# A streaming encoder layer on one core: the new frames' attention in batches of 512 cached keys, the time mixing without a loop

## The reference, cut to what matters

```python
def rwkv_scan(S0, r, w, k, v, kk, a):
    def step(S, inp):
        r_t, w_t, k_t, v_t, kk_t, a_t = inp
        sa = jnp.einsum('bhvk,bhk->bhv', S, -kk_t)
        S = (S * w_t[:, :, None, :] + sa[..., None] * (kk_t * a_t)[:, :, None, :]
             + v_t[..., None] * k_t[:, :, None, :])
        return S, jnp.einsum('bhvk,bhk->bhv', S, r_t)

def fox_sample_attention(q, k, v, logf, k_past, v_past, logf_past):
...
    lp = logf_past.astype(f32)
    tail = jnp.swapaxes(lax.cumsum(lp, axis=1, reverse=True) - lp, 1, 2)
    s_past = (jnp.einsum('bqhd,bkhd->bhqk', q, k_past.astype(q.dtype)).astype(f32) * SCALE
              + c_new[..., :, None] + tail[..., None, :])
    s_new = (jnp.einsum('bqhd,bkhd->bhqk', q, k).astype(f32) * SCALE
             + c_new[..., :, None] - c_new[..., None, :])
    s_new = jnp.where(jnp.tril(jnp.ones((n, n), bool)), s_new, -jnp.inf)
    p = jax.nn.softmax(jnp.concatenate([s_past, s_new], axis=-1), axis=-1).astype(v.dtype)
    return (jnp.einsum('bhqk,bkhd->bqhd', p[..., :P], v_past.astype(v.dtype))
            + jnp.einsum('bhqk,bkhd->bqhd', p[..., P:], v))
```

## Time and profile before

| | us |
|---|---|
| median of three runs | 4143.74 |
| lowest and highest of the three | 4136.17, 4197.59 |
| the profiled execution | 4199.51 |
| its span, first to last instruction | 4197.7 |

### The profile page before, as it was taken

How to read it: one execution, slowest core, us unless ns; L and a number is a source line. 1 busy time by engine, 2 the same in 40 slices (tenths; PEclk the granted TensorE clock), 3 DMA queues, 4 the chain that set the end, 5 groups by cost and what they waited for, 6 DMA issues and landing times. The chain is left out here.

```text
span 4197.7 us, 81747 instructions
## 1 busy us (share of the span) xinstructions
PE 3837.7 (91%) x30701; PEld 2339.2 (56%) x30702; DVE 1621.2 (39%) x3480; ACT 1007.4 (24%) x1829; POOL 232.7 (6%) x348
## 2 busy tenths in 40 slices
PE   8999989989898989869998988994899999999988
PEld 4444448878788878845554764553333333333333
DVE  1222225656556666657775112336011111111117
ACT  2222223323223333225554121110000000000003
POOL 0000010000000000001110000000000000000005
PEclk9999989999999999979999569996899999999999
DMA  5111120000000000021101132220756656754238
GB/s 201 53 53 53 49 56 2 17 10 17 10 10 17 10 17 10 10 97 51 51 11 49 50 105 77 87 84 15 282 216 273 265 208 261 285 225 185 110 116 313
DMA packets 143285, 420.98 MB, mean 100 GB/s; under 512 B 30744, under 2 KB 73888, under 8 KB 130752
## 3 DMA queue, kind: packets, MB, share of 16 engines
q1 hardware_dynamic: 123472, 345.77, 22.4%
q0 software_dynamic: 11616, 42.21, 2.8%
q10 hardware_dynamic: 7952, 29.36, 1.8%
HBM read 750.60 MB, written 69.36 MB: 195 GB/s over the span
## 5 line engine op out<-in xcount | busy, mean ns | idle before, releaser
L2698 PE MATMUL e_H<-e_w,e_xT 128*64 128x512 f32 x1536 | 686.3, 600 | 19.8 <-DMA e_w<-in_moe_w 16.4
L2699 PE MATMUL e_H<-e_w,e_xT 128*64 x1536 | 686.1, 600 | 0.0
L292 PE MATMUL fp<-f_w,f_xT 128*128 128x512 f32 (+1 forms) x1360 | 533.3, 547 | 9.7 <-DMA f_w<-in_w_in 9.3
L716 PE MATMUL rp_pa<-r_xT,w_rwkv 128*128 128x128 f32 x3808 | 484.0, 281 | 0.7 <-ACT r_xT L1020 0.7
L716 PEld LDWEIGHTS rp_pa<-r_xT,w_rwkv 128*128 128x128 f32 x3808 | 449.9, 193 | 35.3 <-issue 23.0
L2698 PEld LDWEIGHTS e_H<-e_w,e_xT 128*64 128x64 f32 x1536 | 208.1, 138 | 436.2 <-issue 409.6
L292 PEld LDWEIGHTS fp<-f_w,f_xT 128*128 128x128 f32 x1360 | 244.2, 199 | 262.6 <-issue 260.9
L2717 PE MATMUL e_Y<-e_w,e_gT 128*64 128x512 f32 x768 | 339.8, 595 | 1.0 <-DMA e_w<-in_moe_w 1.0
L2718 PE MATMUL e_Y<-e_w,e_gT 128*64 x768 | 339.8, 595 | 0.0
L2717 PEld LDWEIGHTS e_Y<-e_w,e_gT 128*64 128x64 f32 x768 | 101.3, 137 | 197.2 <-issue 189.6
L2699 PEld LDWEIGHTS e_H<-e_w,e_xT 128*64 128x64 f32 x1536 | 208.1, 138 | 0.6
(11 more groups left out here) (404 smaller groups left out, 5580.0 us busy)
## 6 DMA issues: line engine op xcount, KB each, us to landing
e_w<-in_moe_w SPq DMA_DIRECT2D x288, 2048.0 KB
scratch_ypad<-e_y ACTq DMA_DIRECT2D x48, 512.0 KB, 2.7
scratch_h<-m_h SPq DMA_DIRECT2D x17, 512.0 KB, 2.6
z_h<-scratch_h SPq DMA_DIRECT2D x17, 512.0 KB, 7.9
f_x<-in_x_prompt SPq DMA_DIRECT2D x16, 512.0 KB, 3.8
r_x<-in_x_prompt SPq DMA_DIRECT2D x16, 512.0 KB, 3.8
c_kc<-in_cache_fox_k SPq DMA_DIRECT2D x32, 256.0 KB, 2.6
c_v<-in_cache_fox_v SPq DMA_DIRECT2D x1, 8192.0 KB, 25.2
```

The lines of the kernel that those rows point to most:

```text
L292: mm = eng.matmul(out, xT[:, slot, k, :], w[:, k, a:a + n], start=(k == 0), stop=(k == KD - 1))
L716: mm = eng.matmul(pre_bank(bank)[:, f * P:(f + 1) * P], w[:, d, (i + f) * P:(i + f + 1) * P], xT[:, d, :], start=(d == 0), stop=(d == KD - 1))
L2698: eng.matmul(out[lower, :], xT[:, s, k, lower], w[:, SECOND, k, :], start=on, stop=off)
L2699: mm = eng.matmul(out[upper, :], xT[:, s, k, upper], w[:, bass.ds(place, 1), k, :], start=on, stop=off)
```

## The change

The sample's attention is written anew. Keys come in 8 batches of 4 tiles. For each batch PE makes 16 transposes into four PSUM banks (one per pair of heads), ACT and DVE copy two banks each, and PE makes the scores in four products of 512 columns and 64 rows, two per group of heads, on alternate halves of the output. The forget sums inside a tile come from products with the gates spread over the 32 queries of each head (ACT spreads them); sums over whole tiles are added by DVE with the reduction that also finds the smallest value. The exponent is taken in pieces of 1024 keys. Weights are turned two tiles at a time, copied by DVE, and multiplied with the values so that each head of a group writes its own strip of 32 rows; the division by the total is done at the end on the result. The small loads and the first half of the keys are issued by SP in the prompt's attention; the keys go into the buffer that held the first half of the prompt's queries, keys and sums, and w_out takes the same place later. Loads of w_out move from ACT's queue to SP's. The old parts stand in the kernel before; the new ones are cut to their core:

```diff
@@ rwkv: run
-            with eng.Fori(0, NT // 2 - 2) as j:
-                for slot in (0, 1):
-                    tile(2 * j + slot + 2, slot, j + 1)
-            tile(NT - 2, 0, NT // 2 - 1)
-            tile(NT - 1, 1, NT // 2 - 1)
+            for t in range(2, NT):
+                tile(t, t % 2, t // 2)
@@ fox_prompt
+        shared = keep["shared"]
+        q = [shared[:, 0:SEQ], sb("a_q", [P, SEQ])[:, :]]
+        k = [shared[:, SEQ:2 * SEQ], sb("a_k", [P, SEQ])[:, :]]
...
+                if j == 1:
...
+                        sp.dma_start(keep["c_lf"][:, :, :], io["cache_fox_logf"][0, 0].rearrange("(n p) h -> p n h", p=P))\
+                          .then_inc(keep["sample_loaded"], 16)
+
+            sp.wait_ge(reduced, last_read[PAIRS - 2, NT - 1][1])
+            for n in range(4):
+                sp.dma_start(shared[:, n * SEQ:(n + 1) * SEQ].rearrange("p (n c) -> p n c", c=DG),
+                             io["cache_fox_k"][0, 0].rearrange("(n p) h d -> p n (h d)", p=P)[:, 4 * n:4 * n + 4, :])\
+                  .then_inc(keep["early_keys_loaded"], 16)
@@ fox_sample, SP
+            keys(EARLY)
+            keys(EARLY + 1)
+            values(0)
+            keys(EARLY + 2)
+            keys(EARLY + 3)
+            values(1)
+            for n in (2, 3):
+
+                sp.wait_ge(scored, BATCHES * (n - 1))
+                values(n)
+            sp.dma_start(keep["w_out"], io["w_out"][0].rearrange("(c p) n -> p c n", p=P)).then_inc(keep["w_out_loaded"], 16)
+            sp.wait_ge(turned_done, PAIRS * (EARLY + 3))
+            sp.dma_start(vnew, io["s_v"]).then_inc(vnew_loaded, 16)
@@ fox_sample, PE
+            def tails(b):
...
+                for g in (0, 1):
+                    for n in range(BT):
+                        eng.matmul(score[b % 2][g][:, n * P:(n + 1) * P], gates[:, b * BT + n, g, :], keep["after"][:, :],
+                                   start=(n == 0), stop=False)
+
+            def scores(b):
...
+                for a in range(PAIRS):
+                    eng.wait_ge(*copied(b, a))
+                    half = slice(a % 2 * DH, (a % 2 + 1) * DH)
+                    mm = eng.matmul(score[b % 2][a // 2][half, :], qbd[:, a, :], kT[:, b % 2, a, :], start=False, stop=True)
...
+            for b in range(BATCHES):
+                if b > 0:
+                    tails(b)
+                scores(b)
+                if b + 1 < BATCHES:
+                    turn(b + 1)
+            new_scores()
...
+            def values(d):
...
+                    for h in range(HEADS):
+                        g, s = divmod(h, HG)
+                        at = i * 256 + g * P + s * NEW
+                        mm = eng.matmul(score[1][g][s * NEW:(s + 1) * NEW, 0:DH], pT[0:w, d % 3, at:at + NEW],
+                                        (v[:, n, :] if n < CT else vnew)[:, h * DH:(h + 1) * DH], start=(n == 0), stop=(n == CT))
...
+            turn_p(0)
+            turn_p(1)
+            for d in range(len(p_copied_all)):
+                if d + 2 < len(p_copied_all):
+                    turn_p(d + 2)
+                values(d)
@@ fox_sample, ACT
+            eng.wait_ge(lowest_made, 1)
+            for c in range(PAST // EXP):
+                m = EXP if (c + 1) * EXP < PAST else EXP + NEW
+                for g in (0, 1):
+                    eng.activation(z[:, g, c * EXP:c * EXP + m], z[:, g, c * EXP:c * EXP + m], ACT.Exp, scale=-1.0,
+                                   bias=lowest[:, g:g + 1], accum_out=total[:, g, c:c + 1]).then_inc(exped, 1)
```

More of the change, by code:

```diff
@@ L1650, in scores @@
                             eng.wait_ge(reduced, unit_free[n - 2][e])
-                        eng.matmul(score[n % 2][e][:, 0:m], q[rows, par, t * P:(t + 1) * P],
-                                   k[rows, par, c * 512:c * 512 + m], start=True, stop=True).then_inc(scored, 1)
+                        eng.matmul(score[n % 2][e][:, 0:m], q[par][rows, t * P:(t + 1) * P],
+                                   k[par][rows, c * 512:c * 512 + m], start=True, stop=True).then_inc(scored, 1)
             def turn(j, b, i):
@@ L1955, in _ @@
-            turn(0, 0, 0)
-            with eng.Fori(0, CT // 2 - 1) as j:
-                for s in (0, 1):
-                    turn(2 * j + s + 1, 1 - s, j + s)
-                    keys(2 * j + s, s)
-            turn(CT - 1, 1, CT // 2 - 1)
-            keys(CT - 2, 0)
-            keys(CT - 1, 1)
-            eng.wait_ge(*kact.after("s", CT - 1))
-            keys(CT, 0, past=False)
-            eng.matmul(bank[5][0:NEW, :], zeros[0:NEW, :], v[0:NEW, CT, :], start=True, stop=False)
-            eng.wait_ge(v_loaded, 16)
@@ new lines, in new_scores @@
+            def new_scores():
+                eng.wait_ge(reduced, 2 * (BATCHES - 1))
+                eng.wait_ge(made, 6)
+                for g in (0, 1):
+                    out = score[BATCHES % 2][g]
+                    eng.matmul(out[:, 0:NEW], pick[:, g, :], negc[:, :], start=True, stop=False)
+                    eng.matmul(out[:, 0:NEW], spread[:, :], keep["causal"][0:NEW, 0:NEW], start=False, stop=False)
+                    for i in (0, 1):
+                        mm = eng.matmul(out[i * DH:(i + 1) * DH, 0:NEW], qbd[:, 2 * g + i, :], knew[:, 2 * g + i, :],
+                                        start=False, stop=True)
+                    mm.then_inc(scored, 1)
@@ new lines, in _ @@
+            eng.wait_ge(keep["sample_loaded"], 64)
+            for h in range(HEADS):
+                mm = eng.matmul(score[1][0][0:CT, h:h + 1], lf[:, :, h], keep["ones"][:, 0:1], start=True, stop=True)
+            mm.then_inc(totalled, 1)
+            turn(0)
+            tails(0)
+            eng.wait_ge(tot_copied, 1)
+            for g in (0, 1):
+                mm = eng.matmul(score[1][1][:, g * CT:(g + 1) * CT],
+                                tot[:, g, :], keep["after"][0:CT, 0:CT], start=True, stop=True)
@@ L2015, in keys @@
-            def keys(n, s):
-                eng.wait_ge(*kpe.after("s", n))
-                eng.copy(logit[:, :, bass.ds(n * P, P)], bank[4][:, 0:2 * P].rearrange("p (g t) -> p g t", g=2))\
-                   .then_inc(*kact.done("s"))
-            turned_keys(0, 0)
-            with eng.Fori(0, CT // 2 - 1) as j:
-                for s in (0, 1):
-                    turned_keys(2 * j + s + 1, 1 - s)
-                    keys(2 * j + s, s)
-            turned_keys(CT - 1, 1)
-            keys(CT - 2, 0)
@@ new lines, in copies @@
+            def copies(b):
+                for a in range(1, PAIRS, 2):
+                    eng.wait_ge(turned_done, PAIRS * b + a + 1)
+                    if b > 1:
+                        eng.wait_ge(scored, 2 * (b - 1))
+                    eng.tensor_copy(kT[:, b % 2, a, :], turned[a][:, :]).then_inc(dve_copied, 1)
+            copies(0)
+            eng.wait_ge(summed, 1)
+            eng.tensor_copy(cum[:, :, :], score[1][1][:, 0:2 * CT].rearrange("p (g n) -> p g n", g=2)).then_inc(cum_copied, 1)
@@ L2993, in build @@
         keep = constants(nc, ctx)
-        for name in ("w_rwkv", "w_out"):
+        for name in ("w_rwkv", "w_out", "sample", "early_keys"):
             keep[name + "_loaded"] = ctx.enter_context(nc.semaphore(name + "_loaded"))
```

378 lines of the change are left out of this document (187 added, 191 removed).

## The result

The changed kernel takes **3970.6 us** (median of four runs, 3966.2 to 3976.0) against 4148.9 (4136.2 to 4197.6) beside it: ratio **0.951, 95% interval 0.944 to 0.957**. The forecast was 3982. The profiled execution took 3973.5 us, its span is 3971.7.

The account below looks back on a forecast made before the run. TensorE (PE) was taken to bound nearly all of the program, with the sample attention the odd one. From the profiled 4199.5 us, 51.2 (time mixing) and 166.3 (sample attention) were subtracted, giving 3982 us, range 3925 to 4045.

Parts of the forecast that it names:

- Time mixing, 51.2 us: Time mixing written out without jumps: eleven tiles at 66.4 us each instead of 781.6 us together, saving 51.2 us.
- Sample attention, 166.3 us: Rewritten sample attention: a stage of 82.2 us against 248.5 us, 166.3 us less.
- the wait: Sample attention after the new keys: PE waits some 4.5 us for last reductions, minimum and two exponents.
- duos: Values of the sample attention: two tiles together take 1.3 us, sixteen such pairs 20.8 us.
- the 4.0 us for the slower clock: Sample attention, behind PE's wait for maximum and exponent: a further 4 us for a slower clock.
- Side by side: Sample attention's PE passes: score halves run two together, 0.43 us a pair; value strips nearly four together, 1.3 us per two tiles.
- The 55.8 us between profile and median: Median 55.8 us below the profiled execution, put down to the old key loop's clock; nothing subtracted as that loop is replaced.
- Half clock in the batches: Rival, sample attention's key batches: clock 0.50 doubles PE's 40.5 us, total 4022 us; chance 0.09.
- Nothing side by side: Rival, sample attention: scores cost 13.8 us and values 18.4 us more, total 4014 us; chance 0.09.
- The slower case, straight code outrun: Rival, time mixing: straight code outruns its loading, two stalls in each of 16 tiles, 301 us, total 4283 us; chance 0.02.
- Loads late: Rival, sample attention: at half the load rate last keys and values hold PE some 20 us, total 4002 us; chance 0.03.
- the 55 us elsewhere: Rival: the old runs differ in a stage that is not changed, so the new median is 3927 us; chance 0.10.

Follow-up runs that it names:

- the two one-sided runs: Changed kernel with tiles 2 to 13 of the time mixing looped on PE alone, 4011.3 us; looped on ACT, DVE and POOL only, 3987.4 us.
- the upper group: Kernel before, unchanged: 37 of its 57 runs, between 4188.3 and 4208.1 us; the other 20 lie between 4136.2 and 4154.1 us.
- the two runs above: Changed kernel with score products over all 128 rows, 3981.3 us; with value products of a group's four heads in one strip of 32 rows, 3989.5 us.

## Why the prediction was right, point by point

*Time mixing, 51.2 us.* Its stretch is 54.2 us shorter, the eleven tiles 51.9. The cause was read rightly from the earlier trace rows: the long tiles come from PE's jumps and from nothing else. That PE's code arrives late after a jump, as the prediction took it, no run shows; they show that the stall comes with PE's own jump. The price of 66.4 a tile had put the rest of the looped tiles' excess into the same sum; of the 51 us of the two one-sided runs 14 are the other engines' looped code, about which the prediction said nothing.

*Sample attention, 166.3 us.* The stage was priced at 82.2 and measures 74.5 from PE's first product. Term by term, forecast and measured: start 5.5 and 5.3; batches 42.1 and 40.8; new keys 1.3 and 1.6; the wait 4.5 and 2.9; the first turn and copy, with the slower clock behind the wait, 6.0 and 2.5 (2287.3 to 2289.8); duos 20.8 and 19.8; last keys and output 2.0 and 1.6. The batches' 0.2 us each for waits was not there. Two more terms were mis-sized, the wait and above all the 4.0 us for the slower clock, which had been carried over from a stall of 5.7 us: after 2.9 us PE's clock was low for 3.4 us only. The duo is 1.17, not 1.3, and two gaps by "issue" (0.97 and 0.53 us) make up part of the difference again.

*Side by side.* Pairs for halves, measured at 0.43 us; sets of four for strips at 0.056: the value near was the right choice. The Trainium skill's 2.38 times for three strips (TensorE: Matmul & The Clock Gate, Part 3) would have made the total 2 to 3 us longer than forecast; here four strips take as long as one pass does (0.056 against 0.054 in the earlier trace rows), and the measurement decides.

*Loads.* No wait of PE for keys, values or w_out shows in the stage. That PE had waited 16.4 us for the small loads was read rightly. What the prediction did not see is that w_out was being loaded beside them: with w_out moved, the same loads at the old place cost PE 6.9 us, and having them ahead is worth 10 us.

*The 55.8 us between profile and median.* That nothing was to be subtracted held: the ten runs of the changed kernel lie within 10 us, and the forecast made against the upper group's profile came out right. That the replaced part held the difference is shown by the spread going with it, and not with the time mixing. That it was the key loop's clock fits the clocks that the runs report, and was not seen.

*Rivals.* Half clock in the batches: 1.00, so the rival did not come. But one of the reasons against it, that PE no longer stands for 16 us, does not carry: in the kernel before, the loop stayed at 0.50 with that standing gone. As what sets that loop's clock is open, there is some luck in this point. Nothing side by side: refuted by the two runs above. The slower case, straight code outrun: PE's gaps by "issue" in the tiles stay under 1 us (at most 1.47 in the other profiles of straight code). Loads late and the 55 us elsewhere did not happen.

*Signs.* One of those named for being right was missed: one of the eleven tiles took 69.2 us at clock 0.95, where 67 and 0.97 were the bounds. It has the gap of 0.88 us by "issue" in it, and most other profiles of the straight code have a longer tile near the same place, up to 68.7 us.

## What to carry to other kernels

A loop is dear at its jump on the engine that sets the pace: look for a pair of "issue" gaps at the same place of every turn, and divide by the turns. More work per turn helps, here from 53.4 to 20.8 us by the traces with two jumps instead of five (from 59 to 33 by the medians), and engines that have slack kept their loops at about 1 us a tile. Products that use half or a quarter of the array should be placed so that neighbours write different rows: starts 7 ns apart in the trace tell that it works. A wait named after the last DMA of a group, and a long issue of that DMA, need not make it the cause: look at which packets the queue was moving, and at what a large load on another queue did to them.

## What the runs showed that was not expected

An issue of a 64 KB load held SP for 12.38 us while its queue was still moving the 4096 small pieces of the load ahead; issued first, the same load took 0.34 us. A kernel whose loop ran at the lower clock in some runs and, by all signs, at the higher one in others was found wholly in the slower group, in ten runs, once 15 us of waiting ahead of it were gone (20 of 57 runs of the kernel before were in the faster one). A batch with three kinds of products on the array takes 0.30 us more than its passes do one by one. With PE alone looped, the tiles without a jump take 65.4 us, less than the 66.3 on average of the written-out ones between 850.2 and 1579.9.
